# Down projection of a mixture of experts: weight pieces by output columns, and the last expert's rows sent back by column halves

## The reference

```python
h2 = rms_norm_2(x, g_ffn[l])
x = x + hier_moe(h2, w_router_g[l], b_router_g[l], w_router_e[l], b_router_e[l], w1[l], w3[l], w2[l])

def hier_moe(h, wg, bg, we, be, w1, w3, w2):
    # each token: the best of 4 groups, then the best 2 of its 8 experts, with gates
    ...
    def expert_block(args):
        xb, e = args
        return (jax.nn.silu(xb @ w1[e]) * (xb @ w3[e])) @ w2[e]
    ys = lax.map(expert_block, (xs, blk_e)).reshape(cap, d)
    ys = ys * gate_buf[:, None].astype(ys.dtype)
    out = jnp.zeros((n + 1, d), ys.dtype).at[tok_buf].add(ys)[:n]
```

## Time and profile before

| | |
|---|---|
| median of 3 executions | 2402.06 us (2401.61 to 2406.68) |
| the profiled execution: its span, first to last instruction | 2390.3 us |
| median less span | 11.8 us |
| PE busy | 2240.4 us (94%) |
| DVE busy | 1375.2 us (58%) |
| ACT busy | 563.7 us (24%) |
| granted TensorE clock, mean | 0.967 |

### The profile page before, as it was taken

How to read it: one execution, slowest core, us unless ns; L and a number is a source line. 1 busy time by engine, 2 the same in 40 slices (tenths; PEclk the granted TensorE clock), 3 DMA queues, 4 the chain that set the end, 5 groups by cost and what they waited for, 6 DMA issues and landing times.

```text
span 2390.3 us, 29072 instructions
## 1 busy us (share of the span) xinstructions
PE 2240.4 (94%) x10734; PEld 1630.0 (68%) x10734; DVE 1375.2 (58%) x3525; ACT 563.7 (24%) x1375; POOL 64.7 (3%) x65
## 2 busy tenths in 40 slices
PE   8988889999999998999999999999799899899987
PEld 6864568888888885558888888888557533333332
DVE  6559857666566657996665666765776311211114
ACT  2013342100011205772100010301583211211110
POOL 0000000000000000000000000000000011111110
PEclk9998799999999999999999999999899799999999
DMA  5220022222323320002332222333004799999997
GB/s 201 88 80 7 17 72 73 87 87 88 88 89 88 126 64 25 1 1 71 88 87 86 85 88 85 100 88 88 1 1 179 276 418 414 418 417 417 418 418 297
DMA packets 69885, 348.11 MB, mean 146 GB/s; under 512 B 10852, under 2 KB 11748, under 8 KB 44208
## 3 DMA queue, kind: packets, MB, share of 16 engines
q1 hardware_dynamic: 64576, 337.13, 38.9%
q0 software_dynamic: 4880, 8.05, 0.9%
q10 hardware_dynamic: 288, 1.05, 0.1%
HBM read 341.00 MB, written 17.30 MB: 150 GB/s over the span
## 4 chain that ended last, share of the span: by engine, by line
PE 71%; DVE 8%; DMA 4%; ACT 3%; issue 2%; DVEq 0%; SPq 0%; ACTq 0%
PE bank L557 26%; PE bank L2458 8%; PE bank L562 7%; PE bank L576 7%; PE bank L569 7%; PE bank L2466 5%; DMA w<-in_experts 4%; PE bank L548 2%; PE bank L2431 1%; DVE exps L1806 1%; PE bank L889 1%; DVE square L2601 1%; PE bank L876 1%; PE bank L901 1%; DVE exps L1996 1%
## 5 line engine op out<-in xcount | busy, mean ns | idle before, releaser
L2458 PE MATMUL bank<-w,xT 128*64 128x512 f32 x960 | 215.6, 598 | 5.7 <-DMA w<-in_experts 4.9
L2631 DVE COPY square<-bank 128x256 f32<-128x256 f32 x32 | 13.6, 425 | 353.1 <-ACT rope L2553 353.1
L2458 PEld LDWEIGHTS bank<-w,xT 128*64 128x64 f32 x960 | 68.3, 138 | 145.4 <-issue 133.1
L1302 ACT ACTIVATE exps<-exps,small 128x128 f32<-128x128 f32 (+1 forms) x224 | 124.3, 559 | 100.2 <-DVE small L1806 99.7
L557 PE MATMUL bank<-u,ring 128*128 128x256 f32 x608 | 143.7, 379 | 0.0
L1576 DVE TENSOR_TENSOR third<-first,bank 128x256 f32<-128x256 f32 x108 | 45.5, 421 | 170.6 <-PE bank L557 169.8
L2466 PE MATMUL bank<-w,square 128*64 128x512 f32 x480 | 131.1, 695 | 5.8 <-ACT square L2560 2.9
L557 PEld LDWEIGHTS bank<-u,ring 128*128 128x128 f32 x608 | 115.4, 190 | 16.5 <-issue 1.0
L557 PE MATMUL bank<-h,ring 128*128 128x256 f32 x512 | 120.9, 379 | 0.0
L557 PE MATMUL bank<-h_sums,w_sum 128*128 128x256 f32 x512 | 120.9, 379 | 0.0
L557 PE MATMUL bank<-u_mlp_sums,w_sum 128*128 128x256 f32 x480 | 113.4, 379 | 0.0
(11 more groups left out here) (442 smaller groups left out, 4228.4 us busy)
## 6 DMA issues: line engine op xcount, KB each, us to landing
w<-in_experts SPq DMA_DIRECT2D x180, 1024.0 KB, 21.1
ring<-in_dense SPq DMA_DIRECT2D x216, 512.0 KB, 3.7
consts<-in_experts SPq DMA_DIRECT2D x12, 1024.0 KB
w<-y_pairs SPq DMA_DIRECT2D x4, 1024.0 KB, 26.8
consts<-in_consts SPq DMA_DIRECT2D x1, 2310.5 KB, 16.5
x<-in_xT SPq DMA_DIRECT2D x4, 512.0 KB, 8.0
h_tokens<-u SPq DMA_DIRECT2D x4, 512.0 KB, 2.8
bias_scratch<-y_ab SPq DMA_DIRECT2D x4, 320.0 KB, 2.4
```

The source lines that it names most:

```text
L1302: act.activation(e, e, ACT.Exp, bias=neg[:, a:a + 1], scale=-1.0, accum_out=total[:, a:a + 1]).then_inc(s[done], 1)
L2458: ins = k.pe.matmul(bank[a * CAP:(a + 1) * CAP, :], xT[:, kk % 4, kk // 4, :], w[:, (2 * (kk % 2) + a) * EH:(2 * (kk % 2) + a + 1) * EH], ...
```

## The change

Each of the two down pieces now holds half of the output columns (256 of the 512 of each half `a`) for all four chunks of inner features, where it held all output columns for two chunks. `pe_down` runs four chunks x 2 halves of 256 columns for each piece, so one column half of bank 5 is complete after the first piece. For the last expert alone, ACT copies the first column half when the first piece is used (`o_first`), PE then sends that half back (`pe_last_columns(0)`, eight products of 256 columns), then uses the second piece, and sends the second half back; DVE adds 16 tiles of 256 columns in place of 8 of 512, and a block goes out when its second half is added. The arithmetic is the same.

```diff
-    down = i["w2_2"][0].reshape(NE, EH // P, P, D).transpose(0, 2, 1, 3).reshape(NE, P, 2, PIECE)
+    down = i["w2_2"][0].reshape(NE, EH // P, P, 2, 2, D // 4).transpose(0, 2, 4, 1, 3, 5).reshape(NE, P, 2, PIECE)
...
@@ moe_tensor
-    pe_last(k, NE - 1)
...
-def pe_down(k, bank, hT, w, c):
-
-    for a in range(2):
-        ins = k.pe.matmul(bank[a * CAP:(a + 1) * CAP, :], hT[:, c % 2, c // 2, :], w[:, c % 2 * D + a * T:c % 2 * D + (a + 1) * T],
-                          start=c == 0, stop=c == EH // P - 1)
+def columns_of(i):
+
+    return slice(i * D // 4, (i + 1) * D // 4)
+
+
+def pe_down(k, bank, hT, w, i):
+
+    n = D // 4
+    for c in range(EH // P):
+        for a in range(2):
+            ins = k.pe.matmul(bank[a * CAP:(a + 1) * CAP, columns_of(i)], hT[:, c % 2, c // 2, :], w[:, (2 * c + a) * n:(2 * c + a + 1) * n],
+                              start=c == 0, stop=c == EH // P - 1)
     return ins
...
@@ pe_expert
             wait_piece(k, e - 1, 4 + i)
-            for c in (2 * i, 2 * i + 1):
-                ins = pe_down(k, k.bank[5], k.hT, k.w[piece(k, e - 1, 4 + i)], c)
-            ins.then_inc(s["w_used"], 1)
+            pe_down(k, k.bank[5], k.hT, k.w[piece(k, e - 1, 4 + i)], i).then_inc(s["w_used"], 1)
+            if e == NE:
+                pe_last_columns(k, i)
...
+def pe_last_columns(k, i):
+
+    pe, s, q, at = k.pe, k.s, LAST - 1, 2 * NB * (LAST - 1) + 2 * NB * i
+    pe.wait_ge(s["o_first" if i == 0 else "o_done"], 1 if i == 0 else NE)
+    for b in range(NB):
+        for a in range(2):
+            j = at + 2 * b + a
+            r = slice(a * CAP, (a + 1) * CAP)
+            pe.wait_ge(s["last_done"], j - 3)
+            pe.matmul(k.bank[LAST_BANKS[b % 2][a]][:, columns_of(i)], k.ST[q][r, b * P:(b + 1) * P], k.oN[(NE - 1) % SETS][r, columns_of(i)],
+                      start=True, stop=True).then_inc(s["last_out"], 1)
...
@@ act_out
+    if e == NE - 1:
+        act.wait_ge(s["w_used"], USED[e, 4])
+        act.activation(k.oN[j][:, columns_of(0)], k.bank[5][:, columns_of(0)], ACT.Copy, scale=k.mt[e % (2 * SETS)][:, 2:3]).then_inc(s["o_first"], 1)
+    act.wait_ge(s["w_used"], USED[e, 5])
...
@@ moe_vector
-    dve_last(k, NE - 1)
-    dve.wait_ge(s["last_done"], 2 * NB * LAST)
+    dve_last_columns(k)
+    dve.wait_ge(s["last_done"], 2 * NB * (LAST + 1))
...
+def dve_last_columns(k):
+    dve, s, at = k.dve, k.s, 2 * NB * (LAST - 1)
+    for i in range(2):
+        for b in range(NB):
+            for a in range(2):
+                j = at + 2 * NB * i + 2 * b + a
+                xt = k.xtok[:, b, a * T + i * D // 4:a * T + (i + 1) * D // 4]
+                if i == 0:
+                    dve.wait_ge(s["paired"], 2 * b + 2)
+                dve.wait_ge(s["last_out"], j + 1)
+                dve.tensor_tensor(xt, xt, k.bank[LAST_BANKS[b % 2][a]][:, columns_of(i)], ALU.add).then_inc(s["last_done"], 1)
...
@@ moe_out
-        eng.wait_ge(s["last_done"], 2 * NB * (LAST - 1) + 2 * (b + 1))
+        eng.wait_ge(s["last_done"], 2 * NB * LAST + 2 * (b + 1))
```

More of the change, by code:

```diff
@@ L2228, in moe_buffers @@
     s.new("sig_exp", "sig_log", "sig_ready", "taken", "both", "hid_done", "hid_turned", "hidT_done", "o_done", *(f"scattered{j}" for j in range(SETS)))
-    s.new(*(f"pairs_in{b}" for b in range(NB)), "paired", "last_turned", "last_ready", "last_done", "last_out", "out_added", "out_done")
+    s.new(*(f"pairs_in{b}" for b in range(NB)), "paired", "last_turned", "last_ready", "last_done", "last_out", "o_first", "out_done")
     late = list(range(SLOTS - LATE, SLOTS))
@@ L2586, in act_out @@
     act, s, j = k.act, k.s, e % SETS
-    act.wait_ge(s["w_used"], USED[e, 5])
     if e >= SETS:
         act.wait_ge(s[f"scattered{j}"], 16 * (e // SETS))
-    act.activation(k.oN[j], k.bank[5], ACT.Copy, scale=k.mt[e % (2 * SETS)][:, 2:3]).then_inc(s["o_done"], 1)
+    if e == NE - 1:
+        act.wait_ge(s["w_used"], USED[e, 4])
+        act.activation(k.oN[j][:, columns_of(0)], k.bank[5][:, columns_of(0)], ACT.Copy, scale=k.mt[e % (2 * SETS)][:, 2:3]).then_inc(s["o_first"], 1)
+    act.wait_ge(s["w_used"], USED[e, 5])
+    gate = k.mt[e % (2 * SETS)][:, 2:3]
+    if e < NE - 1:
+        act.activation(k.oN[j], k.bank[5], ACT.Copy, scale=gate).then_inc(s["o_done"], 1)
+    else:
+        act.activation(k.oN[j][:, columns_of(1)], k.bank[5][:, columns_of(1)], ACT.Copy, scale=gate).then_inc(s["o_done"], 1)
 def dve_slots(k, e):
@@ L2672, in dve_last @@
                 dve.wait_ge(s["last_done"], i - 2 * NB + 1)
-            if q == 2:
-                dve.wait_ge(s["paired"], 2 * b + 2)
             dve.wait_ge(s["last_out"], i + 1)
             dve.tensor_tensor(xt, xt, k.bank[LAST_BANKS[b % 2][a]], ALU.add).then_inc(s["last_done"], 1)
+def dve_last_columns(k):
[9 more added lines that the diff above has]
+                dve.tensor_tensor(xt, xt, k.bank[LAST_BANKS[b % 2][a]][:, columns_of(i)], ALU.add).then_inc(s["last_done"], 1)
 def dve_first_of_equals(k, onehot, values, best, tmp, mr, n):
@@ L2845, in fallback @@
     pe.wait_ge(s["f_act"], 5)
-    for cc in range(EH // P):
-        ins = pe_down(k, k.bank[5], k.hT, k.w[4 + cc // 2], cc)
+    for i in range(2):
+        ins = pe_down(k, k.bank[5], k.hT, k.w[4 + i], i)
     act.wait_ge(s["f_pe"], done.link(ins))
```

## The result

The changed kernel took 2409.15 us, the kernel before 2400.53 us (medians of 19 runs each, 2399.64 to 2418.87 and 2391.34 to 2406.68). The ratio is 1.004, with a 95% interval of 1.0027 to 1.0052: about 9.6 us slower (6.5 to 12.5); the two medians themselves are 8.6 us apart. The forecast was +6.0.

A forecast was written before the change was run, and what follows sets the result against it. Weight loading bounds up to about 2365 us, then gapless DVE the end. PE's added wait, partly at half clock, and the output tail (+6.5 or +5.0, taken +6.0) gave 2402.06 + 6.0 = 2408.1 us; range 2403.8 to 2410.4.

The forecast's parts named there:

- The number: Whole kernel: 2402.06 + 6.0 = 2408.1 us, range for 8 in 10 2403.8 to 2410.4; slower 0.70.
- The bound: At the end, gapless DVE gates expert 31, not the late piece; an earlier product gains zero.
- The wait added: PE's fifth product back waits for DVE's first column add, about 4 us, with the last piece's products queued behind.
- The clock: PE idle before the last piece's products: half clock at restart, full clock back 4.6 us later.
- The output: Output tail: 8.44 us after first issue gives +6.5, 4.88 us after last add gives +5.0; +6.0 taken.
- The adds: Expert 31 on DVE: sixteen adds for eight, nothing added beyond the sum; the second half's eight take 2.80 us.
- The 256-column steps: Down products, experts 0 to 30: 0.213 us a step, no cost; rival, instruction-bound, 2408.5 to 2411, chance 0.08.
- The clock up: Rival: full clock when the last piece's products run; +4.7 or +3.1 us, 2405.2 to 2406.8; chance 0.20.
- The wait that does not bite: Rival: PE does not stop at the fifth product back; last add 0.6 us later, 2402.7; chance 0.04.
- The last piece late: Rival: the last piece, not DVE, gates the end; faster by at most 3.9 us, 2398.2; chance 0.04.

The follow-up runs named there:

- by DVE's order: Changed kernel, DVE adding scattered rows of blocks 0 and 1, then the first column half's eight tiles, then the rest; ratio 1.0024, tail 22.3 us.
- by PE's: Changed kernel, PE using both last down pieces of expert 31 before sending either column half back; ratio 1.0017, tail 22.6 us.
- the kernel whose PE was kept busy: Changed kernel plus seven needless 512-column products into unused bank 0, ahead of PE's fifth product back; ratio 1.0035, tail 24.4 us.
- the one with 1.8 us: Column pieces, both last pieces first, products back, adds and output block by block, scattered rows in full; ratio 1.0005, tail 20.9 us.
- the three kernels without the scattered rows: Kernel before, changed kernel, and order by blocks, scattered-row adds cut to 8 columns; PE's first last-piece step to end 17.2, 18.1, 15.0 us.
- the layout alone: Kernel before with the new down pieces and new `pe_down`, end as before; ratio 1.0014, timed again 1.0000.
- the gain of 2.2 us: Column pieces, both first, output block by block, scattered-row adds cut to 8 columns, against the kernel before with that cut; 15.0 against 17.2 us.
- the kernel before with the same sums: Kernel before, with GpSimd summing the two scattered rows of blocks 0 and 1; ratio 0.9987, tail 19.8 us.

## Why the prediction was right

**The number.** In part luck. The measured 2409.15 us lies within the stated 2403.8 to 2410.4, but that range stood on 2402.06 us, a median of 3 executions, and the kernel before has 2400.53 over 19. As a difference the range was +1.7 to +8.3 us; the timed +9.6 (6.5 to 12.5), or +8.6 by the medians, lies just above it, with an interval that reaches into it. What the traces can check, the tail, came out at +6.7 for the forecast's +6.0, and that is the mechanism's part.

**The bound.** Right. DVE without a gap gates expert 31 in both kernels; the first half was at hand 6.2 us before DVE came (product back at 2388.12, 0.73 us until DVE can add it, first add at 2395.07), and that gained nothing: 9.70 us against 9.71. That the last piece was no gate shows in its steps, which waited for no DMA.

**The wait added.** Right in place and, in the profile, in size. From the first half's first add to the second's were 7.17 us, forecast 7.03. Its parts: until the last piece's steps start 2.91 us (2.52 forecast at half clock), their run and the way to ACT 3.00 (2.98 + 0.29), copy and hand-over 0.53 (0.43), product to add 0.73 (0.81). Undoing the wait's cause alone, by DVE's order or by PE's, took 3.8 or 3.6 us of the 6.7 out of the tail (22.3 and 22.6 us for 26.1), so the cause is shown and not only argued. The timed ratios point the same way (1.0040, then 1.0024 and 1.0017), with intervals that overlap. The wait itself, 6.29 us, was longer than the 4 us I named: the first four products were back 3.9 us after the scattered rows' first add, where I had 6.2, because the piece came 1.4 us sooner against DVE and its steps ran at full clock. That cost nothing, since the wait's end is DVE's.

**The clock.** The level and the return were right: 0.50 at the restart, back 4.5 us later (forecast 4.6). What came before differed: I had left open at which level the first piece runs (1.7 to 3.4 us). It ran at full clock (1.95 us), behind an idle time of 1.43 us and not 2.83 as before, and the clock fell only during the wait on DVE. The price, 1.7 us, is shown by the kernel whose PE was kept busy.

**The output: the term that was mis-sized.** I took +6.0, between +6.5 (8.44 us after the first issue) and +5.0 (4.88 us after the last add), although I wrote that the rows are nearer to the first. Measured, the end came 8.5 us after the first issue and 6.5 us after the last add. By the first rule the forecast's own numbers give +6.5; the tail shows +6.7. From the first issue to the end were 8.0 to 8.7 us in every kernel whose blocks followed one another by 0.7 to 1.6 us on average, and 9.6 us in the one with 1.8 us.

**The adds.** Right: the second half's eight adds took 2.73 us (2.80 forecast). The Trainium skill ("VectorE: DVE Perf Modes", section on the TRN2 errata) gives a fixed latency for each instruction. Set end to end, lengths by its formula would make 3.4 us, an estimate; in this trace the length of one is that of the page, but the next starts 0.33 us after it, (2.73 - 0.42)/7.

**The 256-column steps.** Right: 960 instructions of 256 columns take 130.0 us, 480 of 512 took 131.1, and an expert takes 13.80 us (13.79 before). The group of down products in the kernel before, then in the changed one (busy, mean ns of one), and the changed kernel's rhythm in the timeline:

```profile
L2466 PE MATMUL bank<-w,square 128*64 128x512 f32 x480 | 131.1, 695 | 5.8 <-ACT square L2560 2.9 <-DMA w<-in_experts 2.8
```

```profile
L2472 PE MATMUL bank<-w,square 128*64 128x256 f32 x960 | 130.0, 430 | 4.4 <-ACT square L2579 2.9 <-DMA w<-in_experts 1.4
```

```profile
2186.03 0.44 PE L2496 MATMUL bank<-consts,rope 128*128 128x128 f32 x2
...
2199.83 0.44 PE L2496 MATMUL bank<-consts,rope 128*128 128x128 f32 x2
```

**The rivals.** The clock up: excluded by the 0.50 (its +4.7 is +4.6 by its own sum, 2385.71 + 9.23 - 2390.3). The wait that does not bite: excluded by the 6.29 us. The last piece late: excluded in this profile; its premise, that DVE is free, was set up in the three kernels without the scattered rows, and there too the change lost 0.9 us, so even that wouldn't have made it faster. Its gain of up to 3.9 us was counted to the last add, but from there to the end are 6.5 us with halves and 4.9 without.

**What stays open.** The timed +9.6 us (6.5 to 12.5) include the tail's +6.7, and the 2.9 us between the two are not explained. Six of the seven other timings with the new layout lie above their tails, by 0.5 to 3.5 us, which might be a small cost upstream of the end. The second timing of the layout alone, at 1.0000, speaks against it, and the profiles show none that their spread would not hide: from the issue of the token rows to DVE's first add of expert 30 it was 496.1 to 501.9 us in the four profiles without the new layout (median 497.3) and 496.8 to 504.1 in the ten with it (median 497.7). An interval of 0.2% is as wide as the question.

## What to carry to other kernels

Before giving an engine its input earlier, look whether it has a gap there at all; if it is gapless up to the place, the gain is zero whatever comes sooner. A product split in two so that its first half can leave early must not stand in an in-order queue ahead of the second half's work, if the first half's way out needs buffers that a busy engine frees. And where the output is a few equal transfers that follow one another fast, count the end from the first issue, not from the last result; that rule ends where the results come more slowly than the transfers. A pair of runs that is built to isolate one cause is read with the granted clock beside it: without DVE's load it moved the loss of 0.9 us and the gain of 2.2 us by about 0.8 us each, by the estimate above.

## What the runs showed of the hardware

**Executions of one program differ by 15 us (2391 to 2407 in the 19 of the kernel before; one of a later timing took 2415.5), and the granted clock upstream has a part in it.** The changed kernel's profile was 13.3 us late before the first expert. Compared instruction by instruction with the kernel before, 8.5 us of that were there by 1719 us, and nearly all of the rest came between 1730 and 1750 us. The stretches there, of the kernel before, of the changed one, and of the second profile of the kernel before:

```profile
1734.00:1744.00 10.00, 8.71 (x36) 5.39 (x35) 8.73 (x23) 8.53 (x19) 0.00 (x0) 1.00 0.00 0
1744.00:1754.00 10.00, 10.00 (x39) 5.97 (x38) 6.15 (x15) 8.41 (x17) 0.00 (x0) 1.00 0.00 0
```

```profile
1734.00:1744.00 10.00, 8.34 (x32) 6.55 (x32) 2.70 (x6) 1.14 (x3) 0.00 (x0) 0.52 0.01 2
1744.00:1754.00 10.00, 9.44 (x24) 5.83 (x23) 7.39 (x21) 7.40 (x16) 0.00 (x0) 0.50 0.00 0
```

```profile
1734.00:1744.00 10.00, 9.43 (x23) 5.76 (x22) 6.43 (x20) 6.66 (x14) 0.00 (x0) 0.50 0.00 0
1744.00:1754.00 10.00, 10.00 (x37) 6.20 (x37) 5.70 (x15) 7.29 (x15) 0.00 (x0) 0.91 0.00 0
```

In the two late executions PE, though busy for over 80% of the stretch, was granted 1.2 GHz for 20 us at a time. The third block is the very same program as the first and lies between. Its token rows went out 4.3 us later than in the first, and nearly all of that arose here:

```profile
1873.39 4.74 SPq L2336 DMA_DIRECT2D h_tokens<-u  x4
```

From there to DVE's first add of expert 30 it lost another 5.0 us: between 1910 and 1950 us its loads ran at 364 GB/s and its granted clock was 0.83, against 418 GB/s and 0.96 in the first profile. Which of the two brought the other isn't shown. Why the clock is withheld in one execution and not in the next isn't settled either. That it needs no edit is shown by this pair, and two more kernels without the new layout sent their token rows as late as the changed one (1882.4): at 1880.3 and 1884.7 us.

**The last transfer.** The output ends with one DMA engine of 16 at work (share 0.05 to 0.09) for the last 2 us, in the kernel before and in the changed one.

**An add on GpSimd.** An add of 128 x 1024 took GpSimd 2.4 us (4.83 for two) where DVE needs 1.23. GpSimd was done at 2365.61, 0.12 us before DVE took up expert 30's adds, and DVE did nothing in between (in the kernel before with the same sums they overlap by 0.04 us), so no run shows what the two do to each other side by side.
